# Decode sums, query rotation and the third key block moved in VectorE's order, and the samples' convolution rows summed once

## The reference

```python
def partial_rope(x, pos):
    ...
    out = jnp.concatenate([x1 * cos - x2 * sin, x2 * cos + x1 * sin, rest], axis=-1)

def deltanet_branch(qkv_in, conv_buf, s0, beta_in, a_in, conv_w, a_log, dt_bias, onorm_w):
    ext = jnp.concatenate([conv_buf.astype(qkv_in.dtype), qkv_in], axis=1)
    conv = extf[:, 0:t] * wf[0]
    for i in range(1, CONV_WIDTH):
        conv = conv + extf[:, i:i + t] * wf[i]
    ...
```

## Time and profile before

| | |
|---|---|
| median of 3 runs | 1229.63 us (1226.6 to 1229.8) |
| the profiled execution | 1229.78 us |
| its span, first to last instruction | 1227.9 us |
| TensorE busy | 1181.0 us (96%) |
| VectorE busy | 801.2 us (65%) |
| ScalarE busy | 530.9 us (43%) |
| GpSimd busy | 304.6 us (25%) |
| mean granted TensorE clock | 0.994 of full speed |

### The profile page before, as it was taken

One profiled execution on the slowest core, in us unless ns is written; L12 is line 12 of the kernel. 1 busy time (PEld: TensorE's weight loads), 2 busy tenths in 40 slices (PEclk: granted clock), 3 DMA queues, 4 the chain that ended last, 5 costly groups with the idle time before them and its releaser, 6 DMA issues.

```text
span 1227.9 us, 25153 instructions
## 1 busy us (share of the span) xinstructions
PE 1181.0 (96%) x8553; PEld 1099.6 (90%) x8553; DVE 801.2 (65%) x1945; ACT 530.9 (43%) x1416; POOL 304.6 (25%) x275
## 2 busy tenths in 40 slices
PE   4999999999999999999999999999999999999997
PEld 4899998899889988988898889888988898999996
DVE  5487567756775677577757775777577657465544
ACT  6444345534553445344534463446344635531211
POOL 1124112411241124112312231223122412322211
PEclk9899999999999999999999999999999999999999
DMA  7332543254315432543254325432543264232253
GB/s 244 91 96 72 157 149 104 63 158 147 105 62 162 144 106 62 167 137 112 60 166 138 109 63 168 138 104 63 172 134 121 71 240 152 83 98 88 83 208 140
DMA packets 79645, 151.54 MB, mean 123 GB/s; under 512 B 12353, under 2 KB 22242, under 8 KB 77986
## 3 DMA queue, kind: packets, MB, share of 16 engines
q1 hardware_dynamic: 78254, 148.78, 38.3%
q10 hardware_dynamic: 1312, 1.59, 0.5%
HBM read 132.20 MB, written 17.27 MB: 122 GB/s over the span
## 4 chain that ended last, share of the span: by engine, by line
PE 83%; DVE 9%; ACT 3%; issue 2%; DMA 1%; DVEq 0%; SPq 0%; ACTq 0%
PE PJ L621 20%; PE PJ L617 10%; PE PJ L618 10%; PE PJ L619 10%; PE PJ L622 10%; PE MX L810 2%; PE MX L819 1%; PE MX L731 1%; DVE memx L1596 1%; PE PJ L949 1%; PE MX L751 1%; PE PJ L625 1%; PE MD L888 1%; PE PJ L950 1%; PE PJ L951 1%
## 5 line engine op out<-in xcount | busy, mean ns | idle before, releaser
L621 PE MATMUL PJ<-h,w_hi 128*128 128x512 f32 x1110 | 420.1, 414 | 0.0
L1990 POOL TENSOR_TENSOR w_lo<-w_raw,w_hi 128x512 fp32r<-128x512 f32 x160 | 215.1, 1344 | 813.8 <-ACT w_hi L1022 813.7
L617 PE MATMUL PJ<-h,w_hi 128*128 128x264 f32 (+1 forms) x1216 | 357.2, 294 | 0.0
L618 PE MATMUL PJ<-h,w_hi 128*128 128x264 f32 (+1 forms) x1216 | 345.8, 284 | 0.0
L619 PE MATMUL PJ<-h,w_lo 128*128 128x264 f32 (+1 forms) x1216 | 345.7, 284 | 0.0
L622 PE MATMUL PJ<-h,w_lo 128*128 128x256 f32 x1110 | 310.9, 280 | 0.0
L621 PEld LDWEIGHTS PJ<-h,w_hi 128*128 128x128 f32 x1110 | 208.9, 188 | 43.3 <-DVE w_lo L1402 1.7
L1022 ACT ACTIVATE w_hi<-w_raw 128x512 fp32r<-128x512 f32 x320 | 197.7, 625 | 91.2 <-PE PJ L619 79.1
L618 PEld LDWEIGHTS PJ<-h,w_hi 128*128 128x128 f32 x1216 | 230.8, 190 | 2.3
L617 PEld LDWEIGHTS PJ<-h,w_hi 128*128 128x128 f32 x1216 | 230.5, 190 | 0.0
L619 PEld LDWEIGHTS PJ<-h,w_lo 128*128 128x128 f32 x1216 | 229.4, 189 | 0.0
(11 more groups left out here) (340 smaller groups left out, 1797.9 us busy)
## 6 DMA issues: line engine op xcount, KB each, us to landing
w_raw<-in_w_in SPq DMA_DIRECT2D x256, 256.0 KB, 2.7
w_raw<-in_w_out SPq DMA_DIRECT2D x64, 256.0 KB, 2.8
kv<-in_cache_win_k SPq DMA_DIRECT2D x24, 512.0 KB, 4.8
kv<-in_cache_win_v SPq DMA_DIRECT2D x16, 512.0 KB, 4.4
out<-memx SPq DMA_DIRECT2D x16, 260.0 KB, 3.9
mem<-in_x_prompt SPq DMA_DIRECT2D x4, 1024.0 KB, 10.0
S<-in_state_delta SPq DMA_DIRECT2D x8, 512.0 KB, 3.5
out<-S SPq DMA_DIRECT2D x8, 512.0 KB, 3.0
```

The lines of the kernel that those rows point to most:

```text
L617: pe.matmul(ps, wh, h_hi[:, k, tok], start=k == 0, stop=False)
L618: pe.matmul(ps, wh, h_lo[:, k, tok], start=False, stop=False)
L621: pe.matmul(both, wh, h2[:, :, k, tok], start=k == 0, stop=False)
L1990: pool.tensor_tensor(w_lo[:, par, 4 * q:4 * q + 4, :], w_raw[:, q, :, :], w_hi[:, par, 4 * q:4 * q + 4, :].bitcast(F32), ALU.subtract).the ...
```

## The change

It has four parts.

1. At the start, the products of the samples' three cached rows with their weights are made for all 24 (head, q/k/v) pairs and summed: one product and one reduction. In each convolution the sample columns then take one instruction in place of four. The q convolution (j = 2) does all its 512-column passes in one step.
2. The rotation of q is cut in three: cosine product at step 42, sine product at 43, sum and transpose at 46. The rotation of k has its sum one step later than its products.
3. The value sums L1843 and L1846 go from steps 42 and 46 to 48 and 49, and TensorE's L927 from 48 to 50.
4. The third key block goes to steps 62 and 63 of its own head.

```diff
+        st_prod = gx[:].rearrange("p a t -> p (a t)")[:, 0:9 * NH * NB].rearrange("p (m b i) -> p m b i", m=3 * NH, i=3)
...
             def attn_out(h):
-                yield from idle(46)
+                yield from idle(47)
                 sp.wait_ge(s["q_row"], h + 1)
...
-                yield from idle(7)
+                yield from idle(6)
                 sp.wait_ge(s["k_ok"], h + 1)
...
-                stretch(h, [tail_a(h - 1), attn_decode(h - 1, sums=24, norm=7), own_a(h), mix_b(h), mix_q(h),
+                stretch(h, [tail_a(h - 1), attn_decode(h - 1, sums=26, norm=7), own_a(h), mix_b(h), mix_q(h),
                             delta_decode(h)])
...
-            def rope_on(x, swapped, n, ok):
-
-                t = acc[0:ROT, :]
+            def rope_cos(x):
+                link(dve.tensor_tensor(acc[0:ROT, :], x[0:ROT], rope[:, 0, :], ALU.mult))
+
+            def rope_sin(swapped, n):
                 dve.wait_ge(swapped, n)
-                link(dve.tensor_tensor(t, x[0:ROT], rope[:, 0, :], ALU.mult))
                 link(dve.tensor_tensor(swap, swap, rope[:, 1, :], ALU.mult))
-                dve.tensor_tensor(x[0:ROT], t, swap, ALU.add).then_inc(ok, 1)
+
+            def rope_sum(x, ok):
+                dve.tensor_tensor(x[0:ROT], acc[0:ROT, :], swap, ALU.add).then_inc(ok, 1)
 
             def own_a(h):
                 first = isinstance(h, int) and h == 0
-                yield from idle(44)
-                rope_on(xa, s["q_swap"], 32 * h + 32, s["q_ok"])
+                yield from idle(42)
+                dve.wait_ge(s["proj_sb"], 16 * h + 12)
+                rope_cos(xa)
+                yield
+                rope_sin(s["q_swap"], 32 * h + 32)
+                yield from idle(3)
+                rope_sum(xa, s["q_ok"])
                 dve.wait_ge(s["q_ok"], h + 1)
...
-                yield from idle(7)
-                rope_on(xk, s["k_swap"], 32 * h + 32, s["k_ok"])
-                yield
+                yield from idle(5)
+                dve.wait_ge(s["proj_sb"], 16 * h + 14)
+                rope_cos(xk)
+                rope_sin(s["k_swap"], 32 * h + 32)
+                yield
+                rope_sum(xk, s["k_ok"])
...
-                        if i == (2, 2, 1)[j]:
+                        if i == (2, 2, 3)[j]:
                             yield
-                    st = w[:, 0:24].rearrange("p (b i) -> p b i", i=3)
-                    link(dve.tensor_scalar(acc[:, TP:TT], st[:, :, 0], w[:, 24:25], None, ALU.mult))
-                    for i in range(1, CW):
-                        src = st[:, :, i] if i < 3 else xq[:, 3 + TP:3 + TT]
-                        ins = dve.scalar_tensor_tensor(acc[:, TP:TT], src, w[:, 24 + i:25 + i], acc[:, TP:TT],
-                                                       ALU.mult, ALU.add)
-                        link(ins)
+                    link(dve.scalar_tensor_tensor(acc[:, TP:TT], xq[:, 3 + TP:3 + TT], w[:, 27:28], w[:, 0:NB], ALU.mult,
+                                                  ALU.add))
...
             def decode_keys(h):
...
-                for n in range(2):
+                for n in range(3):
                     yield from key_block(h, n)
-                    yield
+                    if n < 2:
+                        yield from idle((1, 3)[n])
...
-            def last_keys(hh, at):
-
-                yield from idle(at)
-                yield from key_block(hh, 2)
...
+            dve.wait_ge(s["st_sb"], 3)
+            rows = stT[:, :, 0:24].rearrange("p m (b i) -> p m b i", i=3)
+            link(dve.tensor_tensor(st_prod, rows, stT[:, :, 24:27].unsqueeze(2).to_broadcast((P, 3 * NH, NB, 3)), ALU.mult))
+            dve.tensor_reduce(stT[:, :, 0:NB], st_prod, AX.X, ALU.add).then_inc(s["memset_ok"], 1)
...
-                            last_keys(h - 1, 8), attn_decode(h - 1, sums=(22, 4, 3)), decode_keys(h)])
+                            attn_decode(h - 1, sums=(28, 1, 2)), decode_keys(h)])
...
-            work = [last_keys(NH - 1, 4), later(tail_a(NH - 1)), attn_decode(NH - 1, late=-10)]
+            work = [later(tail_a(NH - 1)), attn_decode(NH - 1, late=-10)]
...
                 if isinstance(h, int) and h == 0:
-                    pool.wait_ge(s["st_sb"], 3)
+                    pool.wait_ge(s["memset_ok"], 3)
```

More of the change, by code:

```diff
@@ L1861, in _ @@
             with repeat(dve, 1, NH) as h:
-                ch.at(h, 1, 62)
+                ch.at(h, 1, 53)
                 stretch(h, [tail_a(h - 1), mix_b(h), own_b(h), own_a(h), mix_q(h), delta_decode(h),
-                            last_keys(h - 1, 8), attn_decode(h - 1, sums=(22, 4, 3)), decode_keys(h)])
+                            attn_decode(h - 1, sums=(28, 1, 2)), decode_keys(h)])
             ch.end(NH - 1)
```

## The result

The changed kernel took 1233.21 us (median of 11 runs, 1229.61 to 1236.23), the kernel before 1228.0 us in its runs beside them (11 runs, 1226.27 to 1229.8). The ratio is 1.0041, with a 95% interval of 1.0028 to 1.0055: it became slower by 0.4%. The prediction was 1224.9 us and faster: 4.9 us less than 1229.8, the profiled execution of before, which itself lies 1.8 us above these runs' median. Against 1228.0 it is 5.2 us more where 4.9 less was forecast. The profiled execution of the changed kernel took 1233.21 us, with a span of 1231.4 us at a mean granted clock of 0.987; before, the span was 1227.9 us at 0.994. In the changed kernel the lines after the diff's first additions stand a few lines lower: L810 is L812, L906 is L908, L927 is L929, L731 is L733, L949 is L951, L1683 is L1690, L1715 is L1722, L1788 is L1795, L1846 is L1849.

What follows compares the result with a forecast made beforehand. TensorE's matmul stream at full clock was taken as the bound, so only its holes could be won: 19.7 - 5.8 - 3.0 - 4.4 - 1.6 = 4.9 us, giving 1224.9 us, range 1214 to 1232.

Steps and rivals of the forecast that it cites:

- the sum: Whole kernel: 19.7 us of closed holes less 5.8, 3.0, 4.4 and 1.6 of new waits, 4.9 us gained.
- Value sums: L927 moved to step 50: a new hole of about 0.43 us in seven heads, cost 3.0, bounds 0 and 8.
- L798 and L810: TensorE's holes at steps 30 and 46: closing 0.90 and 1.83 us a head gains 6.3 and 13.4 us.
- L906: Step 43, cosine product ahead of L1788: L906 0.76 us later in seven heads, about 0.5 in the first; cost 5.8.
- Third key block: Steps 62 and 63: L731 0.4 us late at five boundaries, first 0.6, second 1.8, sum 4.4; after last head 1.6.
- Rival C: Head boundaries: key block waits for its load ahead of L1715, slower, 1245 us; chance 0.1 shared with another rival.
- Rival B: Holes only move: L906, L927 and keys cost 0.9 each a head, end 1.6; 21.4 us against 19.7, 1231.5; chance 0.15.

Runs made afterwards that it cites:

- the run where the wait was gone: Changed kernel with VectorE's two value sums one step earlier (47 and 48), L929 still at step 50: 1224.87 us, ratio 0.9968.
- the fastest kernel: Parts 1 and 2 on the kernel before, with the cosine product at step 41; value sums and key block as before: 1210.23 us, ratio 0.9853.

## Why the prediction was wrong

- **The step that failed** is the sum's silence on the clock: "Value sums" priced L927's new place by its wait alone, 3.0 us, and the head was costed at 1.00 throughout, as the earlier trace rows show it. The edit cost 15.8 us on the kernel before and 14.6 on the changed one. Without a fall it is 0.68 a head (122.98 against 122.30) or 0.67 (120.69 with the key block back against 120.02 with the sums back too), 4.7 in seven. Nearly all of the rest is TensorE's clock, at 1.2 GHz for 3.4 us behind the group in four to six of the heads. It is shown by the same edit alone, by its undoing, and by a place one step later that has none. It isn't the chance of single executions: the mean granted clock was 0.983 to 0.990 in the 15 executions of the changed kernel and of the sums alone, and 0.991 to 0.996 in the 8 with the sums back or one step later. That it is the neighbourhood of L831 and L835 that matters is the reading that fits these runs; only the place is shown.
- **Value sums, the wait.** 0.43 was forecast and 0.37 seen in the waits; the head is 0.67 longer. With the wait gone and L929 in its place, a head without a fall takes 120.38 to 120.53, as with the sums back (120.30 to 120.58). So all of the 0.67 went with the wait, though the row shows 0.37 of it; where the other 0.3 lies stays open.
- **L798 and L810.** Both holes are closed, as forecast, but for the first head's 0.5 at L810, which stayed where 0.6 was to be won. Parts 1 and 2 as in the change take a head from 122.30 to 120.02; with L908's 0.70 added back that is 2.98 won, where 0.90 and 1.83 make 2.73.
- **L906.** 0.76 forecast, 0.70 measured (0.86 - 0.16), seven times. The mechanism was right: L1794 is held until GpSimd's piece ends. The 0.5 of the first head did not come.
- **Third key block.** 0.4 a boundary forecast, 0.31 measured in two pairs of kernels; the long wait at the second boundary came as 1.7 for 1.8; the end's wait grew by 1.5 for 1.6. Alone it cost 4.3 us where 6.0 stood in the sum. In that run the long wait at the second boundary is absent: its waits have no row for L731. Rival C did not come.
- **The heads add up.** 122.30 - 1.02 (part 1) - 1.26 (part 2, with L908's cost) gives the 120.02 of both parts. With the 0.68 of the sums and the 0.31 of the keys, each measured alone on the kernel before, it is 121.01; the changed kernel's one head without a fall or a long wait takes 121.00.
- **Not foreseen at the end:** a wait of 1.2 to 1.8 us for L1958, in every kernel with part 1 and in none without it. Just ahead of it VectorE stands idle for 1.5 to 2.1 us, and TensorE's wait is 0.2 to 0.3 less than that in each of the ten; why VectorE stands there, and only with part 1, stays open. And a fall behind the start of the output projection: in all six of the kernels above with L951 or L949 waiting 2.9 or 3.0 there, and in one of the others.
- Rival B's time (1231.5) was near the result, but not its reason: the waits took about the 15 us of the gain that the forecast gave them (4.9 for L908, 4.7 for the sums, some 5.2 for the keys), and the clock the rest.

What stays open is why one head has a fall and its neighbour none. In the head without a fall of the changed kernel the group looks the same:

```profile
372.71 1.95 PE L929 MATMUL MD<-ones,kv 128*128 128x1 f32 x16 [0.37 <-DVE kv L1849]
```

with the same 0.37 ahead, and the clock behind it is 1.00. The five falls start 122.9 us apart each time, although the heads between them take 122.5 to 122.8, so they start 2.4 us behind L929's start in one head and 3.2 in another: their instants don't follow the heads. Whether that decides which head has one was not tried.

## What to carry to other kernels

When a change moves a group of small matmuls, read what stands next to it on TensorE as well as its wait: here one-column matmuls right ahead of other small ones were followed by half the clock for some us, and that cost more than the wait. Cost each part by the length of an undisturbed head rather than by the sum of waits; lengths added to 0.01 us here where medians mixed two effects. And look where the profiled execution lies among the others before its falls are counted. Of this change keep parts 1 and 2, with the cosine product one step earlier: 1210.23 us, 1.5% faster than before, with no new hole in the heads but 0.3 at L908.

## What the runs showed of the hardware

- TensorE's granted clock fell to 1.2 GHz in a span in which TensorE was 96% busy, for 3.4 us, and twice for 6.8 in the value sums alone. In the two falls shown TensorE was busy for 3.03 of the 3.40 us just ahead. The Trainium skill, "TensorE: Matmul & The Clock Gate", section "A second HAM failure mode: psum-queue depth-cycling", tells of another kernel whose clock swings between its two levels because short idle times lie between its groups of matmuls. The trace agrees in that no long idle time was needed: 0.37 us stood ahead of the group, and none directly ahead of it in the run where the wait was gone.
- A VectorE instruction of 8 columns can take 1.13 to 1.51 us beside a GpSimd one, and which of two linked ones is hit changes with a shift of hundredths of a us: in the fastest kernel one head had L1795 hit (1.05 us) in place of L1794 (0.16), with the starts of L1794 and of the GpSimd piece 0.01 us apart instead of 0.02, and was 0.32 us shorter (119.35 against 119.67).
